# Second block of a two-block model: what follows the token mixing for 256 columns in place of 272

## What is computed

```python
h_res = concat([meta(16), x(256)])                     # 272 tokens
h = rmsnorm(h_res, norm1_w)
q, k, v, z, b, a, sc_b, sc_c, sc_x, gate_a, gate_b = split(h @ w_in)
o_dn = gated_deltanet_bidir(q, k, v, z, b, a, ...)     # mixes tokens; ends in norm(o) * silu(z)
y_a = o_dn @ w_branch_dn
y_b = (sc_b * conv3(sc_c * sc_x)) @ w_branch_sc        # conv3 mixes neighbours
merged = sigmoid(gate_a) * y_a + sigmoid(gate_b) * y_b
h_res = h_res + merged @ w_out
gu = rmsnorm(h_res, norm2_w) @ w_gate_up               # 2 * 2816 columns
h_res = h_res + (silu(gu[:, :2816]) * gu[:, 2816:]) @ w_down
return rmsnorm(h_res, final_norm_w)[:, 16:]
```

## Time and profile before

| | us |
|---|---|
| three runs | 1517.66, 1518.50, 1519.98 |
| median | 1518.5 |
| span of the profiled execution | 1512.8 |
| median less span (start and end of the program) | 5.7 |
| PE busy in that span | 1356.0 (90%) |
| DVE busy | 860.9 (57%) |
| ACT busy | 671.8 (44%) |
| POOL busy | 265.1 (18%) |
| mean share of the 16 DMA engines, stream queue | 36.1% |

### The profile page before, as it was taken

One profiled execution on the slowest core, in us unless ns is written; L12 is line 12 of the kernel. 1 busy time (PEld: TensorE's weight loads), 2 busy tenths in 40 slices (PEclk: granted clock), 3 DMA queues, 4 the chain that ended last, 5 costly groups with the idle time before them and its releaser, 6 DMA issues.

```text
span 1512.8 us, 32274 instructions
## 1 busy us (share of the span) xinstructions
PE 1356.0 (90%) x12138; PEld 1288.6 (85%) x12138; DVE 860.9 (57%) x1352; ACT 671.8 (44%) x1067; POOL 265.1 (18%) x259
## 2 busy tenths in 40 slices
PE   4889989979899989899658799999999899799997
PEld 4878978979799978898548789989989899799997
DVE  4334745546436645555488866666657565555544
ACT  5334435433434445433434553333333453566633
POOL 0000040006000220152042225336235000000000
PEclk9999989989999989999788999999999999999999
DMA  4524543334444523344223332231221454355553
GB/s 184 189 90 154 180 153 112 111 103 161 135 139 142 192 97 125 104 161 140 96 84 107 116 112 79 77 98 59 94 80 61 150 177 144 120 175 172 174 189 110
DMA packets 55481, 194.71 MB, mean 129 GB/s; under 512 B 6248, under 2 KB 9832, under 8 KB 54640
## 3 DMA queue, kind: packets, MB, share of 16 engines
q1 hardware_dynamic: 49248, 179.33, 36.1%
q10 hardware_dynamic: 5856, 13.30, 2.5%
q0 software_dynamic: 304, 1.07, 0.2%
HBM read 189.26 MB, written 4.41 MB: 128 GB/s over the span
## 4 chain that ended last, share of the span: by engine, by line
PE 61%; issue 22%; DVE 8%; ACT 3%; DVEq 2%; POOL 1%; POOLq 1%; DMA 1%; ACTq 0%
PE stream_ps L277 16%; PE stream_ps L279 15%; PE stream_ps L278 15%; DVE w_lo L269 2%; DVE qkvT L1099 2%; PE free_ps L1655 1%; PE free_ps L1638 1%; ACT w_hi L263 1%; PE free_ps L355 1%; PE free_ps L1656 1%; DVEq L1105 1%; POOLq L407 1%; PE free_ps L1403 1%; DMA cst<-cst_dram 1%; DVE oT L362 1%
## 5 line engine op out<-in xcount | busy, mean ns | idle before, releaser
L277 PE MATMUL stream_ps<-h_hi,w_hi 128*128 128x256 f32 (+1 forms) x2016 | 603.0, 299 | 54.8 <-DVE w_lo L269 25.6
L269 DVE TENSOR_TENSOR w_lo<-raw,w_hi 128x1024 fp32r<-128x1024 f32 x342 | 431.4, 1268 | 347.9 <-ACT w_hi L263 341.6
L279 PE MATMUL stream_ps<-h_hi,w_lo 128*128 128x256 f32 (+1 forms) x2016 | 585.6, 290 | 0.0
L278 PE MATMUL stream_ps<-h_lo,w_hi 128*128 128x256 f32 (+1 forms) x2016 | 585.5, 290 | 0.0
L277 PEld LDWEIGHTS stream_ps<-h_hi,w_hi 128*128 128x128 f32 x2016 | 393.4, 195 | 66.2 <-issue 31.9
L278 PEld LDWEIGHTS stream_ps<-h_lo,w_hi 128*128 128x128 f32 x2016 | 392.8, 195 | 0.7 <-issue 0.5
L279 PEld LDWEIGHTS stream_ps<-h_hi,w_lo 128*128 128x128 f32 x2016 | 392.7, 195 | 0.0
L263 ACT ACTIVATE w_hi<-raw 128x1024 fp32r<-128x1024 f32 x342 | 358.6, 1054 | 61.8 <-PE stream_ps L279 55.3
L1222 DVE TENSOR_TENSOR xy<-xy,free_ps 64x128 f32<-64x128 f32 x180 | 44.7, 283 | 62.7 <-PE free_ps L1656 47.4
L1099 DVE SCALAR_TENSOR_TENSOR qkvT<-st_raw,gains,qkvT 128x272 f32<-128x272 f32 x96 | 65.8, 726 | 5.3 <-ACT qkvT L681 2.6
L794 ACT ACTIVATE n<-free_ps 64x128 f32<-64x128 f32 x80 | 22.0, 275 | 105.2 <-PE free_ps L1638 104.3
(11 more groups left out here) (327 smaller groups left out, 2141.6 us busy)
## 6 DMA issues: line engine op xcount, KB each, us to landing
raw<-stream_dram SPq DMA_DIRECT2D x342, 512.0 KB, 3.5
gate_spill<-gate_out ACTq DMA_DIRECT2D x16, 136.0 KB, 2.0
xT<-xT_dram ACTq DMA_DIRECT2D x1, 1088.0 KB, 8.8
stage<-wik_dram ACTq DMA_DIRECT2D x2, 544.0 KB, 4.9
x_spill<-xT ACTq DMA_DIRECT2D x1, 1088.0 KB, 4.0
gb<-gate_spill ACTq DMA_DIRECT2D x1, 1088.0 KB, 7.0
ga<-gate_spill ACTq DMA_DIRECT2D x1, 1088.0 KB, 9.2
xT<-x_spill ACTq DMA_DIRECT2D x1, 1088.0 KB, 5.7
```

Of the source, the lines that this page charges most:

```text
L269: nc.vector.tensor_tensor(w_lo[s][:, :, :], raw[:, s, :].rearrange("p (k n) -> p k n", k=KT), w_hi[s][:, :, :].bitcast(F32), ALU.subtract) ...
L277: nc.tensor.matmul(ps, l_hi, r_hi, start=first, stop=False)
L278: nc.tensor.matmul(ps, l_hi, r_lo, start=False, stop=False)
L279: return nc.tensor.matmul(ps, l_lo, r_hi, start=False, stop=last)
```

## The change

All of stage 3 from sc_b on, and stages 4 to 9, take the slices of 256 columns. sc_c and sc_x keep 272, since the convolution needs the neighbour of column 16. The tiles `ga`, `gb`, `yd_*`, `ys_*`, `f_*`, `gate_out` and `bcv` become 256 wide, `h32t` is replaced by `oS` after the first norm, and `sz` becomes the first 256 columns of `xT`. The DRAM buffers `x_spill` and `gate_spill` keep rows of 272, of which 256 are written and read. No instruction is added, removed or moved.

```diff
-                ga, gb = (sb(n, [P, KT, T], scope=br2) for n in ("ga", "gb"))
+                ga, gb = (sb(n, [P, KT, S], scope=br2) for n in ("ga", "gb"))
...
+        oS = oT[:, :, TP - S:]
-        sz = xT
+        sz = xT[:, :, 0:S]
...
-            act.dma_start(a["x_spill"], xT[:, :, :]).then_inc(x_out, 16)
+            act.dma_start(a["x_spill"][:, :, tok], xS).then_inc(x_out, 16)
...
-                nc.scalar.activation(gate_out[:, :], stream_ps[s % 2][:, 0:T], ACT.Tanh, scale=0.5).then_inc(act_evac, 1)
+                nc.scalar.activation(gate_out[:, :], stream_ps[s % 2][:, 0:S], ACT.Tanh, scale=0.5).then_inc(act_evac, 1)
...
-            act.dma_start(gb[:, :, :], a["gate_spill"][:, KT:, :]).then_inc(gb_in, 16)
-            act.dma_start(ga[:, :, :], a["gate_spill"][:, 0:KT, :]).then_inc(ga_in, 16)
+            act.dma_start(gb[:, :, :], a["gate_spill"][:, KT:, 0:S]).then_inc(gb_in, 16)
+            act.dma_start(ga[:, :, :], a["gate_spill"][:, 0:KT, 0:S]).then_inc(ga_in, 16)
...
-                nc.scalar.activation(ys_hi[:, ks, :], cx[:, ks, 1:T + 1], ACT.Copy).then_inc(yshi_ready, 1)
+                nc.scalar.activation(ys_hi[:, ks, :], cx[:, ks, NM + 1:T + 1], ACT.Copy).then_inc(yshi_ready, 1)
...
-            act.dma_start(xT[:, :, :], a["x_spill"]).then_inc(x_back, 16)
+            act.dma_start(xS, a["x_spill"][:, :, tok]).then_inc(x_back, 16)
...
-                    xt = xT[:, bass.ds(4 * w + s, 1), :].rearrange("p a n -> p (a n)")
-                    nc.vector.tensor_tensor(xt, stream_ps[s][:, 0:T], xt, ALU.add).then_inc(dve_evac, 1)
-            split_norm(3 + LAYERS, G_NORM2, 2 * LAYERS + 2)
+                    xt = xS[:, bass.ds(4 * w + s, 1), :].rearrange("p a n -> p (a n)")
+                    nc.vector.tensor_tensor(xt, stream_ps[s][:, 0:S], xt, ALU.add).then_inc(dve_evac, 1)
+            split_norm(3 + LAYERS, G_NORM2, 2 * LAYERS + 2, oS, xS, hS_hi, hS_lo)
...
-                block_part(s, ks)
+                block_part(s, ks, *((h_hi, h_lo) if s < 2 else (hS_hi, hS_lo)))
...
-                    mm = mm3(stream_ps[s % 2][:, 0:T], w_hi[s][:, k, :], w_lo[s][:, k, :], h_hi[:, k, :], h_lo[:, k, :],
+                    mm = mm3(stream_ps[s % 2][:, 0:hi.shape[-1]], w_hi[s][:, k, :], w_lo[s][:, k, :], hi[:, k, :], lo[:, k, :],
...
-                        mm = mm3(stream_ps[c][:, 0:T], w_hi[s][:, k, :], w_lo[s][:, k, :], f_hi[:, kf, :], f_lo[:, kf, :],
+                        mm = mm3(stream_ps[c][:, 0:S], w_hi[s][:, k, :], w_lo[s][:, k, :], f_hi[:, kf, :], f_lo[:, kf, :],
```

More of the change, by code:

```diff
@@ L187, in build @@
             with ExitStack() as br2:
-                ga, gb = (sb(n, [P, KT, T], scope=br2) for n in ("ga", "gb"))
[L189 to L192, removed]
+                ga, gb = (sb(n, [P, KT, S], scope=br2) for n in ("ga", "gb"))
+                yd_hi, yd_lo, ys_hi, ys_lo = (sb(n, [P, KT, S], F32R, br2) for n in ("yd_hi", "yd_lo", "ys_hi", "ys_lo"))
+            f_hi = sb("f_hi", [P, FT, S], F32R, two)
+            f_lo = sb("f_lo", [P, FT, S], F32R, two)
+            f_act, f_val = (sb(n, [P, 2, S], scope=two) for n in ("f_act", "f_val"))
         h32p = oT
         h32t = oT[:, :, TP - T:]
-        sz = xT
+        oS = oT[:, :, TP - S:]
+        sz = xT[:, :, 0:S]
         vs = vb[:, :, :].rearrange("p h (d c) -> p h d c", d=2)
@@ L825, in _ @@
                 for h in range(4):
-                    op = nc.scalar.activation(wide[:, 4 * half + h, :], free_ps[h][:, 0:T], ACT.Ln, bias=eps_col[:, 0:1], scale=1.0 / P)
+                    op = nc.scalar.activation(wideS[:, 4 * half + h, :], free_ps[h][:, 0:S], ACT.Ln, bias=eps_col[:, 0:1], scale=1.0 / P)
                 op.then_inc(oss_used, 1)
@@ L845, in _ @@
                 ks = slice(4 * half, 4 * half + 4)
-                nc.scalar.activation(h_hi[:, ks, :], wide[:, ks, :], ACT.Copy, scale=0.5).then_inc(mhi_ready, 1)
+                nc.scalar.activation(hS_hi[:, ks, :], wideS[:, ks, :], ACT.Copy, scale=0.5).then_inc(mhi_ready, 1)
             def squares(G, D_at):
@@ L1285, in _ @@
                     k = bass.ds(4 * w + s, 1)
-                    part, other, merge = (x[:, k, :].rearrange("p a n -> p (a n)") for x in (ga, gb, wide))
+                    part, other, merge = (x[:, k, :].rearrange("p a n -> p (a n)") for x in (ga, gb, wideS))
                     dve.wait_ge(blk_done, SLOTS + 4 * (G_BR + 2 + w) + s + 1)
-                    nc.vector.scalar_tensor_tensor(out=part, in0=part, scalar=1.0, in1=stream_ps[s][:, 0:T], op0=ALU.add, op1=ALU.mult)
+                    nc.vector.scalar_tensor_tensor(out=part, in0=part, scalar=1.0, in1=stream_ps[s][:, 0:S], op0=ALU.add, op1=ALU.mult)
                     nc.vector.drain()
@@ L1699, in _ @@
                     for j in range(4):
-                        mm = nc.tensor.matmul(free_ps[j][:, 0:T], ones, wide[:, 4 * half + j, :], start=True, stop=True)
+                        mm = nc.tensor.matmul(free_ps[j][:, 0:S], ones, wideS[:, 4 * half + j, :], start=True, stop=True)
                     mm.then_inc(oss_done, 1)
```

89 lines of the change are left out of this document (45 added, 44 removed).

## The result

| | before | after |
|---|---|---|
| median (runs, lowest to highest) | 1517.66 (9, 1510.65 to 1522.31) | 1504.72 (9, 1501.21 to 1509.29) |
| ratio, 95% interval | | 0.9917, 0.9896 to 0.9937 |
| profiled execution: time, span, mean clock | span 1512.8, 0.950 | 1507.09, 1505.3, 0.944 |

A forecast was written before the change was run, and what follows sets the result against it. PE, busy for 90% of the span, was taken as the bound. Terms of 0.1 + 4.8 + 3.1 - 0.1 + 0.8 + 7.0 + 4.1 + 0.4 = 20.2 us, off 1518.5, gave 1498.3 (range 1496.5 to 1500.5).

The forecast's parts named there:

- The count and the pace: 2928 matmuls at 256 instead of 272 columns, 118 instead of 126 ns each: 22.8 us if PE never waits more.
- Steps: The five delta-rule steps: narrower matmuls save 4.8 us in all, except where PE waits for `cx`.
- w_out: Output projection: DVE's adds, held by a chain through ACT, go from 3.13 to 3.11 us apart; 0.8 us saved, not 1.5.
- gate/up: Rounds of four blocks go from 12.10 to 11.48 us, ACT and DVE becoming the bound; 7.0 us saved, not 8.2.
- down: Last projection: 528 matmuls save 7.8 ns each, 4.1 us, with ACT and DVE having half that to do.
- end: Final norm's sums, small operations and scalings get shorter, output DMA unchanged: 0.4 us saved.
- Units 0 and 1: Blocks ahead of the first step: PE's saving becomes waiting for DVE, only DVE's four operations shorten; 0.1 us saved.
- Rival (a): Chains through ACT and DVE in w_out and gate/up don't bind, PE bounds everywhere: 24.0 us saved, 1494.5; chance 0.14.
- rival (b): At the branches, 1024-byte DMA pieces hold ACT or `gb` lands late: 1 to 4 us lost, 1499.3 to 1502.3; chance 0.19.
- rival (c): New PE pauses in gate/up bring half clock, 2.8 us more a block, 1622 if all 44 ran so; chance 0.02.
- Their saving turns into wait: In each step, 18 matmuls before PE's wait for `cx` save nothing, except 0.07 us by DVE's shorter chain.
- the rows at 219:227: Profile stretch of 8 us at 1.2 GHz behind a pause of PE, holding about 25 matmuls; cited for the slower-clock rival.

## Why the forecast was wrong

**The count and the pace** were right: 118 to 119 ns at 256 columns. The gap rule of the Trainium skill, TensorE: Matmul & The Clock Gate, "Back-to-back issue gap", by which the change would have brought 6 us, fell; 19.6 came with the clock nearly equal on both sides.

**Steps, w_out, gate/up, down, end** were right in their mechanisms and nearly in size where the clock was 1.00: 1.07 us a step (1.05 forecast), 3.11 us an add, 11.47 us a round (11.48). `sum_squares` at the end takes 3.47 us instead of 3.68, as forecast:

```profile
1492.87 3.47 PE free_ps L356 x16
```

Units 0 and 1 saved 0.45 us and not 0.1; which of their waits gave way is open.

Rival (a), that the rings don't bind, is refuted by the round; rival (b) by the issues and by the landing of `gb`.

**The step that failed** is the clock. The forecast had PE's granted clock as given by the profile of before, with "each stretch at half clock more or less is about 1.5 us" as its whole allowance, and looked for a new one only in gate/up (rival (c)). There the clock did stay at 1.00, after a start at half clock that both kernels have at the same cost, 3.8 us busy (after, after, before):

```profile
1302.30:1425.00 122.70, 122.70 (x1034) 1.00 0.55 179
1292.10:1302.30 10.20, 3.78 (x18) 0.50 0.03 13
```
```profile
1293.20:1300.00 6.80, 3.80 (x17) 0.50 0.00 0
```

So the forecast's sign for (c), a clock under 1.00 between 1290 and 1490, was badly drawn: the kernel before shows it too. Two sentences of its own pointed elsewhere. "Their saving turns into wait" says that PE's pause in each step grows while the work around it shrinks; I put the price of that at the wait alone, 0.1 us, where a stretch costs 3.0 us of a step (62.69 for 59.73, 61.7 for 58.7). And the rows at 219:227 showed that a pause is paid for twice. Right would have been to list every pause of PE in the changed kernel (cx in each step, ys_lo, h_lo twice, f_lo), to ask of each whether it grows, and to give each a chance of a stretch: five steps at 3.0 us, two starts at 1.6. That makes a range of 0 to some 18 us above 1498.3 and not of 3.7. The mechanism of (c) was the right one, and its place was wrong. It took 10.6 of the 20.1 us from the first step on, and not all.

The reading that a matmul takes twice as long at 1.2 GHz was wrong as well. Of the 25 in 219:227 the first twelve are of other shapes; those of 256 columns behind them start 0.21 us apart, as at the start of down, so a block at half clock costs 2.3 us more and not the 2.8 of rival (c).

The Trainium skill has the mechanism: TensorE: Matmul & The Clock Gate, "Part 1: The HAM clock gate", says that a piece of hardware that watches how busy PE has been sets the clock, and that the number of matmuls at half clock changes with the phase at which a kernel meets it. The traces agree: the same 2.5 us ahead of w_out drew a stretch in some kernels and none in others.

**The base** was a little off too. I took the three runs as 5.7 us above the profiled span. Every execution listed since has its time 1.8 to 2.0 us above its span, so the profiled execution took about 1514.6, and 29 runs of the kernel before in the first round of experiments have a median of 1516.65: some 2 us of the 1518.5 were spread.

## What to carry to other kernels

Where PE is the bound, a pause of it can have two prices, the wait and the clock behind it; read the granted clock around each pause before costing a change, and when work next to a pause becomes less, reckon with a lower clock behind it. Here pauses of 0.86 us cost only themselves in 24 of 25 steps. This change saved its full price only with the pauses taken out too: two orders on DVE and ACT and one wait cut in three were worth another 16.6 us by the medians, 19.1 from the first step on. Test an expected saving against a pair of kernels without the pauses, since it may be right and still not show.

## What the runs showed that I had not expected

- Less work on PE alone made the kernel slower: 16 columns fewer in the 144 matmuls of each step (96 in the last) gave 1.0044, where the step times without a stretch (58.7 for 59.7 us, five times) would give 0.997.
- A drain between two pieces of an operation made PE's wait 1.0 us longer, while the two pieces without it changed nothing, and two halves with a second drain right behind each of two others changed nothing either (4.3 us in five steps in both).
